# Moved steps at eleven places where TensorE waits, and ten channel sums as two fp32r passes instead of one fp32 pass

## The reference, cut to what matters

```python
def first_block(x, ...):
    hn = rms_norm(x, norm_mix_g)
    u_mla, u_fox, u_ssm, u_gate = split(hn @ w_in)
    y_a = mla_branch(u_mla) @ w_br_mla     # 8 heads, q and k of 96 channels, rms_norm per head, rope
    y_b = fox_branch(u_fox) @ w_br_fox     # 8 heads of 64 channels, rms_norm per head, decay mask
    y_c = ssm_branch(u_ssm) @ w_br_ssm     # 16 heads, causal conv, chunked scan, rms_norm
    x = x + (g0 * y_a + g1 * y_b + g2 * y_c) @ w_out
    return x + conv_ffn(rms_norm(x, norm_ffn_g))          # 2 x 2816 hidden
def second_block(x, mem, ...):
    x = pool_layer(x, mem)       # trailing means, memory attention, swiglu
    x = sb_layer(x, mem)         # 12 stick-breaking heads, 4 memory heads, swiglu
    return rmsnorm(x, final_norm)
```

## Time and profile before

| what | us |
|---|---|
| median of 3 runs | 1108.15 (1107.95 to 1108.33) |
| the profiled execution's own time | 1107.72 |
| its span (first to last instruction) | 1105.9 |
| PE busy | 1080.5, 98% of the span |
| DVE busy | 815.1, 74% |
| ACT busy | 632.8, 57% |
| POOL busy | 98.7, 9% |
| granted TensorE clock, mean | 0.997 of full speed |
| DMA | 190.97 MB, mean 173 GB/s |

### The profile page before, as it was taken

How to read it: one execution, slowest core, us unless ns; L and a number is a source line. 1 busy time by engine, 2 the same in 40 slices (tenths; PEclk the granted TensorE clock), 3 DMA queues, 4 the chain that set the end, 5 groups by cost and what they waited for, 6 DMA issues and landing times.

```text
span 1105.9 us, 19448 instructions
## 1 busy us (share of the span) xinstructions
PE 1080.5 (98%) x7444; PEld 980.5 (89%) x7444; DVE 815.1 (74%) x1332; ACT 632.8 (57%) x1046; POOL 98.7 (9%) x112
## 2 busy tenths in 40 slices
PE   8999999999999999999999999999999999999997
PEld 8986999999999999988979888888899778888886
DVE  6856898668777999956765888876756447888654
ACT  6675767556657666644335655545567545555453
POOL 0000211056200333300000000000000000000000
PEclk9999999999999999999999999999999999999999
DMA  9345533455545556456426555445643036554451
GB/s 355 142 165 187 209 136 107 173 192 198 183 161 190 177 180 233 154 182 221 162 77 228 177 191 191 165 158 183 233 149 136 17 117 231 188 191 166 166 189 47
DMA packets 33899, 190.97 MB, mean 173 GB/s; under 512 B 3916, under 2 KB 7268, under 8 KB 16676
## 3 DMA queue, kind: packets, MB, share of 16 engines
q1 hardware_dynamic: 33252, 188.95, 48.4%
q10 hardware_dynamic: 576, 1.05, 0.3%
HBM read 187.86 MB, written 2.12 MB: 172 GB/s over the span
## 4 chain that ended last, share of the span: by engine, by line
PE 70%; DVE 16%; ACT 7%; issue 5%; DMA 1%; DVEq 1%; SPq 0%; ACTq 0%
PE bank L949 26%; PE bank L960 14%; PE bank L961 7%; DVE w_lo L1938 7%; DVE acc L2352 3%; PE S L960 3%; PE bank L1009 3%; ACT w_hi L1498 2%; PE O L960 2%; PE T L960 2%; PE S L961 2%; PE bank L1018 1%; PE O L1394 1%; PE O L961 1%; DVE pr L2332 1%
## 5 line engine op out<-in xcount | busy, mean ns | idle before, releaser
L1938 DVE TENSOR_TENSOR w_lo<-ring,w_hi 128x1024 fp32r<-128x1024 f32 (+2 forms) x354 | 379.3, 1113 | 97.9 <-ACT w_hi L1498 96.7
L1498 ACT ACTIVATE w_hi<-ring 128x1024 fp32r<-128x1024 f32 (+2 forms) x354 | 322.6, 961 | 192.7 <-PE bank L949 125.2
L949 PE MATMUL bank<-xhl,w_hi 128*128 128x256 f32 x1792 | 321.0, 282 | 1.9 <-DVE w_lo L1938 1.5
L949 PEld LDWEIGHTS bank<-xhl,w_hi 128*128 128x128 f32 x1792 | 273.4, 188 | 6.3 <-issue 4.9
L949 PE MATMUL bank<-xhl,w_lo 128*128 128x256 f32 x896 | 250.3, 279 | 0.0
L960 PE MATMUL bank<-hid,w_hi 128*128 128x512 f32 x528 | 184.9, 394 | 3.3 <-DVE w_lo L1938 2.9
L949 PEld LDWEIGHTS bank<-xhl,w_lo 128*128 128x128 f32 x896 | 168.8, 188 | 0.0
L961 PE MATMUL bank<-hid,w_lo 128*128 128x256 f32 x528 | 147.8, 280 | 0.0
L960 PE MATMUL bank<-xhl,w_hi 128*128 128x512 f32 x352 | 124.9, 392 | 1.3 <-DVE w_lo L1938 1.2
L960 PEld LDWEIGHTS bank<-hid,w_hi 128*128 128x128 f32 x528 | 99.2, 188 | 28.5 <-issue 6.0
L961 PE MATMUL bank<-xhl,w_lo 128*128 128x256 f32 x352 | 99.3, 282 | 0.0
(11 more groups left out here) (354 smaller groups left out, 1941.1 us busy)
## 6 DMA issues: line engine op xcount, KB each, us to landing
ring<-w_up SPq DMA_DIRECT2D x22, 1024.0 KB, 4.8
ring<-w_upa SPq DMA_DIRECT2D x22, 1024.0 KB, 4.8
ring<-w_upb SPq DMA_DIRECT2D x22, 1024.0 KB, 4.8
ring<-w_gate SPq DMA_DIRECT2D x12, 1024.0 KB, 4.9
ring<-w_down SPq DMA_DIRECT2D x16, 704.0 KB, 4.0
ring<-w_downa SPq DMA_DIRECT2D x16, 704.0 KB, 4.1
ring<-w_downb SPq DMA_DIRECT2D x16, 704.0 KB, 4.2
ring<-w_xbc SPq DMA_DIRECT2D x6, 1024.0 KB, 5.0
```

The costliest lines, as they stand in the source:

```text
L949: last = mm(out, lhs, rhs, start=(start and k == 0 and (a, b) == (0, 0)), **kw, stop=(whole and k == ks[-1] and (a, b) == (1, 0)))
L1498: A(w_hi[:, q % 2, a:e], raw[:, a:e], ACT.Copy).then_inc(hi_ready, 1)
L1938: last = V.tensor_tensor(w_lo[:, q % 2, a:e], raw[:, a:e], w_hi[:, q % 2, a:e], ALU.subtract)
```

## The change

Eight parts; the letters are used from here on.

- **A, warm-up.** 17 instead of 11 matmuls on a tile of ones before the first real one.
- **B, two-pass sums.** For the first ten small norms (`TWO_PASS`) ACT adds an fp32r copy `sqr_h` of the squares, DVE adds `sqr_l = sqr - sqr_h`, and PE sums the two in two fp32r matmuls against `blk_r` or `ones_r`, which ACT makes once, at the step `rest`, ahead of cq's squares. The new tiles lie over `pr` and `pT`.
- **C, m6 and m7.** The norm m6 and the squares of m7 go from tick 0 to tick 1 of the first layer, the norm m7 from tick 1 to tick 2. There it stands behind a Tanh; ACT's queue gets two ACT_TABLE_LOADs more.
- **D, half of brs 1** goes ahead of the ssm norm's last sum.
- **E, fills of the stick-breaking layer.** `qq 1` is whole in tick 1, `kv 1` in ticks 2 and 3, `kk 2` in 4 and 5, `qq 2` whole in 6; the ahead parts are 8 matmuls a tick in ticks 12 and 13, and output group 2 has ahead parts too.
- **F, ffn1 and ffna.** The first half of the slot behind the last squares is split ahead of `high_parts`/`low_parts` of the last group.
- **G, end of ffn1.** Of the last two hidden tiles, which were both DVE's, tile 20 goes to POOL.
- **H, last norm.** POOL multiplies pair 2, DVE the other three; the stores go in the order 0, 1, 3, 2.

```diff
-            out += {0: [("nm", "m6"), ("sq", "m7")], 1: [("nm", "m7")]}.get(t, [])
+            out += {1: [("nm", "m6"), ("sq", "m7")], 2: [("nm", "m7")]}.get(t, [])
...
-    st += [("g", "brs", 0), ("ns", "ssm", 3), ("nm", "ssm")] + [("g", "brs", n) for n in range(1, 4)]
+    st += [("g", "brs", 0), ("half", "brs", 1), ("ns", "ssm", 3), ("nm", "ssm")] + [("g", "brs", n) for n in range(1, 4)]
...
-    more = [sum(both("kk", 1), []), *both("qq", 1), both("kv", 1)[0], both("kv", 1)[1] + both("kk", 2)[0],
-            both("kk", 2)[1] + both("qq", 2)[0], both("qq", 2)[1], *both("kv", 2), *both("qmb", 0)]
-    more += [[("ahead", i, m, 0)] for i in range(2) for m in range(2)]
-    more += [[("ahead", i, m, 4) for m in range(2)] for i in range(2)] + [[]]
+    more = [sum(both("kk", 1), []), sum(both("qq", 1), []), *both("kv", 1), *both("kk", 2), sum(both("qq", 2), []),
+            *both("kv", 2), *both("qmb", 0)]
+    more += [[("ahead", i, m, 0) for m in range(2)] for i in range(2)] + [[("ahead", 2, m, 0)] for m in range(2)]
+    more += [[("ahead", i, m, 4) for m in range(2)] for i in range(3)]
...
+TWO_PASS = SMALL[:-2]
...
-            for i in range(4):
-                sp.wait_ge(normed, NORMED["last"] + i + 1)
+            for n, i in enumerate((0, 1, 3, 2)):
+                sp.wait_ge(*((pool_normed, 1) if i == 2 else (normed, NORMED["last"] + n + 1)))
                 sp.dma_start(out[:, 2 * i * S:2 * (i + 1) * S], flat(x[:, 2 * i:2 * i + 2, :])).then_inc(stored, 16)
...
-                if name in SMALL:
+                if name in TWO_PASS:
+                    m = SMALL.index(name)
+                    lhs = blk_r[:, :] if width == 64 else ones_r[0:QK, :]
+                    pe.wait_ge(sums_in, 2)
+                    pe.wait_ge(sqr_hi, m + 1)
+                    mm(b[:, :], lhs, sqr_h[0:p, m % 2, :], start=True, stop=False)
+                    pe.wait_ge(sqr_lo, m + 1)
+                    last = mm(b[:, :], lhs, sqr_l[0:p, m % 2, :], start=False, stop=True)
+                elif name in SMALL:
...
-            for _ in range(11):
+            for _ in range(17):
                 mm(Ob[:, 0:P], pT[:, 0, 0:P], pT[:, 0, 0:P], start=True, stop=True)
...
                 for wait in input_ready(name, i) if (name, i) != ("last", 3) else ():
                     act.wait_ge(*wait)
+                if name in ("ffn1", "ffna") and i == 3:
+                    split_behind(name, 0)
...
+                    if name in TWO_PASS:
+                        act.wait_ge(squared, n["squared"])
+                        A(sqr_h[0:p, m % 2, :], sqr[0:p, m % 2 * 2 * S:(m % 2 + 1) * 2 * S], ACT.Copy).then_inc(sqr_hi, 1)
...
                     act.wait_ge(rest_in, 32)
+                    A(blk_r[:, :], C("blk"), ACT.Copy).then_inc(sums_in, 1)
+                    A(ones_r[:, :], C("ones"), ACT.Copy).then_inc(sums_in, 1)
...
                     for i in range(4):
                         dve.wait_ge(gained, i + 1)
+                        if i == 2:
+                            continue
...
-                    for j in range(NFF // RING * RING, NFF):
-                        hidden(j, j % RING, j // RING)
+                    dve.wait_ge(hid_t, NFF - 1)
+                    dve.wait_ge(hid_high, NFF - 1)
+                    dve.wait_ge(up_hid, NFF - 1)
+                    hidden(NFF - 1, (NFF - 1) % RING, (NFF - 1) // RING)
...
+                elif s[0] == "sq" and s[1] in TWO_PASS:
+                    m, p = SMALL.index(s[1]), NORMS[s[1]][1]
+                    dve.wait_ge(sqr_hi, m + 1)
+                    V.tensor_tensor(sqr_l[0:p, m % 2, :], sqr[0:p, m % 2 * 2 * S:(m % 2 + 1) * 2 * S],
+                                    sqr_h[0:p, m % 2, :], ALU.subtract).then_inc(sqr_lo, 1)
                 elif s[0] == "sq" and len(s) == 3:
+                    early = s[1] in ("ffn1", "ffna")
+                    if early and s[2] == 3:
+                        behind(s[1], 0)
...
             for s in STEPS:
+                if s == ("nm", "last"):
+                    pool.wait_ge(gained, 3)
+                    pool.wait_ge(rstd_ready, len(NORM_AT))
+                    Q.tensor_tensor(x[:, 4:6, :], x[:, 4:6, :], rstd[:, 0:S].unsqueeze(1).to_broadcast([P, 2, S]), ALU.mult)\
+                        .then_inc(pool_normed, 1)
...
+                    up(NFF - 2, 0, NFF // RING, base)
```

More of the change, by code:

```diff
@@ L557, in build @@
         sc = sb("sc", [P, 2, 384])
+        with ExitStack() as z:
+            sqr_h = z.enter_context(nc.sbuf_tensor("sqr_h", [P, 2, 512], F32R))
+            sqr_l = z.enter_context(nc.sbuf_tensor("sqr_l", [P, 2, 512], F32R))
         pr = sb("pr", [P, 2, 512])
@@ L595, in build @@
         gates3 = mqk[:, 8:16, :]
+        z.close()
+        z, zb = zone()
+        zb("hole6", [P, 45, S])
+        blk_r, ones_r = zb("blk_r", [P, P], F32R), zb("ones_r", [P, P], F32R)
         z.close()
@@ L1149, in group @@
                 elif stage == "brs":
-                    last = feature3(stage, i, 256, two3, after("ssm") if i == 0 else None, (ssm_h, ssm_l))
+                    last = feature3(stage, i, 256, two3, after("ssm") if i == 0 else None, (ssm_h, ssm_l), half)
                 elif stage == "out1":
@@ L1496, in high @@
                     act.wait_ge(*wait_used)
-                for a, e in halves_of(raw.shape[-1]):
+                for m, (a, e) in enumerate(halves_of(raw.shape[-1])):
+                    if half not in (None, m):
+                        continue
                     A(w_hi[:, q % 2, a:e], raw[:, a:e], ACT.Copy).then_inc(hi_ready, 1)
@@ L1504, in head_high, with splits @@
                 A(w_hi[:, 0, a:e], ring[:, 0, a:e], ACT.Copy).then_inc(hi_ready if i % 2 else head_hi, 1)
-            def splits(g, behind=None):
+            def splits(g, behind=None, half=None):
                 for key in split_at(g, behind):
@@ L1620, in high_parts, with split_behind @@
                 last.then_inc(xh_ready, 1)
+            def split_behind(name, half):
+                for g, norm in LAST_PAIR.items():
+                    if norm == name:
+                        splits(g, True, half)
             def squares(name, i=None):
@@ L1667, in squares @@
                     n["wide"] += 1
-                    for g, norm in LAST_PAIR.items():
-                        if norm == name:
-                            splits(g, behind=True)
+                    split_behind(name, 1 if name in ("ffn1", "ffna") else None)
             def norm_rstd(s):
@@ L1932, in copied, with low @@
                 dve.wait_ge(evacuated[g % RING], g // RING + 1)
-            def low(raw, q, it, count):
+            def low(raw, q, it, count, half=None):
                 for m, (a, e) in enumerate(halves_of(raw.shape[-1])):
+                    if half not in (None, m):
+                        continue
                     dve.wait_ge(hi_ready, it * 2 * RING + (2 * count - 1 + m))
@@ L1940, in low @@
                         last.then_inc(head_low, 1)
-                last.then_inc(lo_ready, 1)
+                if half != 0:
+                    last.then_inc(lo_ready, 1)
             def head_rest(i):
@@ L2162, in low_parts, with behind @@
                 last.then_inc(normed, 1)
-            def behind(name):
+            def behind(name, half):
                 for g, norm in LAST_PAIR.items():
                     if norm == name:
-                        splits(g, behind=True)
+                        splits(g, True, half)
             def add_squares(name, i):
@@ L2429, in _ @@
                     if s[2] == 3:
-                        behind(s[1])
+                        behind(s[1], 1 if early else None)
                     if s[1:] == ("mixa", 3):
```

12 lines of the change are left out of this document (8 added, 4 removed).

## The result

The changed kernel takes 1115.22 us (median of four runs, 1114.09 to 1118.33), the kernel before 1108.18. The ratio is 1.0068 with a 95% interval of 1.0050 to 1.0087: slower by about 7 us, outside the forecast range. The profiled execution is the slowest of the four, 1118.33, span 1116.5. One execution of a later kernel (C alone) took 1781.12 at a mean granted clock of 0.558 and is left out of its median.

The account below looks back on a forecast made before the run. PE was taken as the bound, busy 1080.5 of a span of 1105.9. Eight parts summed to +1.75; on 1107.72 plus 0.43 for the median this gave 1110.0 against 1108.15, range 1103.0 to 1113.0.

Parts of the forecast that it names:

- the forecast case: Whole kernel: the parts sum to +1.75, giving 1110.0, with an own range of 1108 to 1112; chance 0.48.
- rival 1: Clock falls behind the waits at f0 and m4, 1.6 each: one gives 1111.6, both 1113.2; chance 0.14.
- a wait of 2.5: Before up of ffnb: the last low parts come at 915.2 where PE wants them at 912.7, +2.5.
- Rival 5: Last norm: POOL and DVE take turns, last multiplication ends 1.5 later, H 1.65 worse than forecast, 1111.6; chance 0.04.
- G's -0.25: End of ffn1: POOL's tile 20 takes 2.5, DVE's last tile waits for it, w_lo starts only 0.25 sooner.
- the term: Ten two-pass sums save 4.0; waits at cq 0.5, f0 1.9, m3 0.35, m4 1.95 take it to +0.7.
- 0.35 of waiting: At m3 the multiplication of m2 stands ahead of DVE's subtraction: +0.35, an estimate.
- no wait: At f1, m0, f2, m1, f3, m2 and m5 the subtraction is in time; the first six save the full 0.40 each.
- brs 3: w_lo of brs 3 ends near 309.55 where PE wants it at 308.95, so 0.6 of D's gain comes back.
- Rival 2: Subtractions and splits are in time, closed waits stay closed: down to 1097.8, milder 1101.7 or 1103.9; chance 0.28.
- Rivals 3 and 4: Table loads cost more (C +2.6, 1112.6), or fp32r passes are slower (B +4.0 at most, 1113.9); together 0.06.
- its own terms (1.75 and 2.3): Stick-breaking layer: early waits going, about -1.75; the 1.42 at 878.83 and what follows closing, -2.3.

Follow-up runs that it names:

- f0 and m4 fed: Kernel before with part B alone, PE given redundant matmuls during its waits at m4 and f0: 1109.34 against 1108.14.
- lower group alone: The four faster of eleven runs of the kernel before with only E's ahead parts: mean 1108.43 against 1108.14.
- four sums and D: Kernel before with 17 warm-up matmuls, two-pass sums at m0, f2, f3, m2 only, and half of brs 1 ahead: 1106.20, ratio 0.9981.
- changed kernel less four pieces: Changed kernel with f0 and m4 in one fp32 pass, E's old ahead parts, and parts G and H undone: 1108.85.
- seven sums: Kernel before with 17 warm-up matmuls, two-pass sums at f1, m0, f2, m1, f3, m2, m5, plus D and F: 1106.70, ratio 0.9985.
- m4 fed: Changed kernel, PE repeating the high pass of m4's sum five times more while waiting for sqr_l: 1115.39.
- B with m4 fed: Kernel before with part B alone, PE given redundant matmuls at m4: two groups of times, 1109.1 to 1110.0 and 1111.0 to 1111.4.
- f0 and m4 in one pass: Changed kernel with the sums of f0 and m4 as one fp32 pass again, the other eight two-pass: 1112.09.

## Why the prediction was wrong

The sign held and so did most of the new waits; the forecast case did not. Step by step, forecast and measured:

| step | forecast | measured | from |
|---|---|---|---|
| B | +0.7 | +1.2 | B alone, f0 and m4 fed |
| C | +1.25 | +1.4 | C alone |
| E, ahead | +0.2 | +0.3 | lower group alone |
| G | -0.25 | +0.6 | wait of 0.59 before `hid`, the 1.07 as before |
| H | -0.15 | +1.0 | 6.7 against 5.7 from DVE's first multiplication to the end |
| D, F, fills of E | 0.0 | +0.5 | -0.3, +0.4, +0.4, see below |
| clock, profiled execution | 0 | +5.6 | 2.6 (m4), 1.6 (ffn1), 1.4 (ffnb) |

The measured column makes the 10.6 between the two profiled executions; that it does so to the last tenth is partly luck, since several terms are good to 0.2 only. The 1.6 is the row at 476.80 against its like with H undone, 2.60 apart, and the row of the pooling layer at 575.77, 4.23 apart: a profile where ffn1's clock held against one where it didn't. The 1.4 is the gap between the two groups with E's ahead parts alone. D, F and the fills of E were not run one by one; their prices are read from how far PE is from the kernel before at the same matmul. With four sums and D it is -1.52 at m6 (107.81 against 109.33) and -1.81 at the end of ffn1 (470.69 against 472.50): D is -0.3. With F too it goes from -0.77 (108.56) to -0.64 (471.86), so F is about +0.4. In the changed kernel less four pieces it goes from +0.59 at 797.97 (797.38 before) to +0.99 at 879.82 (878.83 before): the fills are +0.4.

- **The step that failed first is the clock: the sum has no term for it, and rival 1 was held at 0.14.** "The engine had been busy for 40 us before" was the argument against, and it carried nothing: the clock fell behind 2.33 us of idle time in two pieces after 95 us of work, and behind 0.59 + 1.07 after 470. I also weighed it at f0 and m4 alone, and not at up of ffnb, where the forecast itself had put a wait of 2.5; and at f0 no profile shows it. Its price of 1.6 a fall was about right (1.0 to 2.6 measured). The profiled execution had three falls, and the range's upper end of 1113.0 left out even two (1113.2). Without the clock the steps make +5.0 where +1.75 was forecast, about 1113; the fastest execution of H undone (1111.63, mean clock 0.998) with H's 1.0 gives 1112.6. So the other misses alone reach the range's upper end, and the clock carries the time past it.
- **Rival 5 was right in kind, at both places, and held at 0.04.** At H its price was too high: DVE's last multiplication ends 0.46 later and not 1.5, since POOL's is a row of 1.70 that overlaps DVE's first and not 2.06 behind it, and the end comes 1.0 later with the stores. G's -0.25 counted POOL's 2.5 (2.4 measured) without what it does to DVE and without ACT's `sg` behind it. The Trainium skill ("SBUF — State Buffer", section "SBUF: two separate sides") says that the two take turns for the whole instruction; the DVE rows of 0.96 against 0.47 and 1.75 against 0.69, each ending just behind POOL's, agree.
- **In B the term came out 0.5 too low by f0, m4 and m5.** The 0.40 a sum came at seven places. m3 is among them, where I had put 0.35 of waiting, and that takes back part of what the three cost. f0 cost 1.9 net where the forecast has 1.9 less its own 0.40, m4 cost 1.8 net and not 1.55, and m5's 0.40 went into the next wait. With the wait at f0 gone (seven sums), the low pass came late at f1, m1 and m5, so there "no wait" would have been wrong too.
- **Right:** the places and lengths of the waits at f0 (1.9, was 2.04), m4 (over 2, was 2.33, though 1.51 of it is for ACT's copy, which the forecast does not name), brs 3 (0.6, was 0.52), ffnb (2.5, was 2.31); C at its price; warm-up worth nothing in the sum, as min 1 still waits until 15.46 (15.43 before).
- **Rival 2 is refuted:** behind nearly every closed wait a new one stands in the rows above. Rivals 3 and 4 did not come: the two loads take 1.28 each and nothing more, and the pair at f3 takes 0.46. PE's busy time did not fall by 4: it rose by 3.8, with the three falls in it.
- **Two slips of arithmetic** change nothing: 1107.72 + 1.75 + 0.43 is 1109.9, and with every closed wait of E staying closed its own terms (1.75 and 2.3) give -4.05, not -2.9.

What stays open: why the clock held behind a wait in one execution and fell behind the same wait in another, whether it falls at f0 as the times say, and how often each place falls.

## What to carry to other kernels

Price a closed wait together with the next one on the same engine, and then ask how long the new one leaves TensorE idle: here idle times of 1.6 to 2.3 us cost another 1.0 to 2.6 through the clock in some executions, and with redundant matmuls in the gaps of B alone the long executions were gone at no cost. Work moved to GpSimd beside two-input VectorE work can cost VectorE more than it saves: 0.5 for a GpSimd row of 0.8 to 1.0, 1.1 for one of 1.7. A row of the same VectorE instructions with and without it shows that before anything is changed. A split of fp32 work into high and low passes pays only where the low part is there first and no other wait follows that takes the gain.

## What the runs showed of the hardware that I had not expected

- The granted clock fell behind a wait in some executions and held behind the same wait in others. The single gaps of 1.42 and 1.24 held in every profile that has them. A fall cost 1.0 to 2.6 us. The profiles in which it fell and held:

| TensorE idle | fell | held |
|---|---|---|
| f0, 2.03 to 2.04 | in none | changed kernel, G undone, H undone, m4 fed, B alone, B with m4 fed |
| m4, 1.5 and 0.8 | changed kernel, G undone | H undone, B alone |
| ffn1, 0.6 and 1.1 | changed kernel, m4 fed, f0 and m4 in one pass | H undone |
| ffnb, 2.31 | changed kernel, G undone, H undone, f0 and m4 in one pass, E's ahead parts | m4 fed |

- The last rows of the kernel before and after: three two-input multiplications on DVE beside one on POOL take longer (2.96) than four alone (2.50), all of it in the one that meets POOL's (1.75 against 0.69).
